# Two sums of a branch layer on VectorE, sigmoids ahead of a weight split, and biased attention with bias and row extreme in one operation

## The reference

```python
# na: 16 heads of 64, 256 queries by 256 keys
s = einsum(q, k) * 64 ** -0.5
s = where(col_mask, s + bias, NEG_INF)          # a bias per head
o = softmax(s) @ v
# branches: four branches of the same normed input, summed under sigmoid gates
s_swa = where(window, q @ k * 64 ** -0.5 + rel_bias, NEG_INF)   # 4 heads, softmax with a sink
s_fox = where(causal, q @ k * 64 ** -0.5 + cum_q - cum_k, NEG_INF)   # 4 heads
g = sigmoid(z_gate)                                             # 4 gates of width 1024
merged = g[0] * p_conf + g[1] * p_sc + g[2] * p_swa + g[3] * p_fox
x = x + merged @ w_out
```

## Time and profile before

| | |
|---|---|
| median of 3 runs | 3464.23 us |
| the profiled execution, its time | 3465.64 us |
| its span, first to last instruction | 3463.8 us |
| granted TensorE clock, mean | 0.983 of full |
| PE (TensorE) busy | 3390.5 us, 98% |
| DVE (VectorE) busy | 2606.3 us, 75% |
| ACT (ScalarE) busy | 1653.2 us, 48% |
| POOL (GpSimd) busy | 203.2 us, 6% |

### The profile page before, as it was taken

One profiled execution on the slowest core, in us unless ns is written; L12 is line 12 of the kernel. 1 busy time (PEld: TensorE's weight loads), 2 busy tenths in 40 slices (PEclk: granted clock), 3 DMA queues, 4 the chain that ended last, 5 costly groups with the idle time before them and its releaser, 6 DMA issues. The chain is left out here.

```text
span 3463.8 us, 59540 instructions
## 1 busy us (share of the span) xinstructions
PE 3390.5 (98%) x23844; PEld 3130.5 (90%) x23844; DVE 2606.3 (75%) x2909; ACT 1653.2 (48%) x1753; POOL 203.2 (6%) x156
## 2 busy tenths in 40 slices
PE   8999999999899999999999999999999999999999
PEld 7999998998699998699999989999999999999998
DVE  7778778775677777577877887777778777777876
ACT  4464444443545444444546444544445444444544
POOL 0000012000000000000000000000341000025100
PEclk9999999999899999899999999999999999999999
DMA  6543385554254554155554335455434545553454
GB/s 247 192 182 122 123 230 179 196 183 146 74 199 178 195 188 153 49 192 186 193 192 173 122 124 202 174 193 193 168 137 165 190 184 197 188 183 129 164 196 168
DMA packets 98937, 592.88 MB, mean 171 GB/s; under 512 B 25684, under 2 KB 26836, under 8 KB 27736
## 3 DMA queue, kind: packets, MB, share of 16 engines
q1 hardware_dynamic: 97280, 586.34, 47.5%
q10 hardware_dynamic: 1496, 4.20, 0.4%
HBM read 588.40 MB, written 2.11 MB: 170 GB/s over the span
## 5 line engine op out<-in xcount | busy, mean ns | idle before, releaser
L1654 DVE TENSOR_TENSOR low<-raw,high 128x2048 fp32r<-128x2048 f32 x531 | 1236.8, 2332 | 229.2 <-ACT high L1180 226.7
L1180 ACT ACTIVATE high<-raw 128x2048 fp32r<-128x2048 f32 x550 | 1049.1, 1910 | 654.5 <-PE acc L445 359.1
L574 PE MATMUL wide<-xs,high 128*128 128x512 f32 x3840 | 1339.3, 391 | 5.9 <-DVE low L1654 5.9
L575 PE MATMUL wide<-xs,low 128*128 128x256 f32 x3840 | 1083.4, 282 | 0.0
L574 PEld LDWEIGHTS wide<-xs,high 128*128 128x128 f32 x3840 | 721.4, 188 | 154.6 <-issue 4.0
L575 PEld LDWEIGHTS wide<-xs,low 128*128 128x128 f32 x3840 | 726.5, 189 | 0.0
L443 PE MATMUL acc<-ends,high 128*128 128x256 f32 x2112 | 588.9, 279 | 0.0
L444 PE MATMUL acc<-ends,high 128*128 128x256 f32 x2112 | 588.8, 279 | 0.0
L445 PE MATMUL acc<-ends,low 128*128 128x256 f32 x2112 | 588.8, 279 | 0.0
L443 PE MATMUL wide<-xs,high 128*128 128x256 f32 x1912 | 550.3, 288 | 13.9 <-DVE low L1669 11.4
L444 PE MATMUL wide<-xs,high 128*128 128x256 f32 x1912 | 540.7, 283 | 0.0
(11 more groups left out here) (229 smaller groups left out, 3596.8 us busy)
## 6 DMA issues: line engine op xcount, KB each, us to landing
raw<-stream SPq DMA_DIRECT2D x550, 1024.0 KB, 4.8
work<-rpb SPq DMA_DIRECT2D x16, 256.0 KB, 7.3
work<-bias_shifted ACTq DMA_DIRECT2D x2, 1024.0 KB, 4.8
cst<-consts SPq DMA_DIRECT2D x1, 1050.0 KB, 11.4
x<-x_in SPq DMA_DIRECT2D x1, 1024.0 KB, 4.9
raw<-stream SPq DMA_DIRECT2D x2, 512.0 KB, 7.2
work<-bias_by_distance ACTq DMA_DIRECT2D x2, 512.0 KB, 4.9
bias_shifted<-work ACTq DMA_DIRECT2D x1, 1024.0 KB, 3.9
```

Of the source, the lines that this page charges most:

```text
L574: nc.tensor.matmul(out[:, n, :, :], wh, xs[:, :, k, :], start=(k == 0), stop=False, skip_group_check=True)
L575: last = nc.tensor.matmul(out[:, n, 0, :], wl, xh[:, k, :], start=False, stop=(k == KC - 1), skip_group_check=True)
L1180: nc.scalar.activation(high[:, s % HIGH, :], raw[:, s % RAW, :], ACT.Copy).then_inc(high_ready, 1)
L1654: v.tensor_tensor(low[:, s % LOW, :], raw[:, s % RAW, :], high[:, s % HIGH, :].bitcast(F32), ALU.subtract).then_inc(low_ready, 1)
```

## The change

Four things, in the `na` layer and in both branch layers:

- **Biased attention.** The scale by 1/8 goes into the query gain: `par("na_q")`, `swq` and `fxq` are multiplied once, by five operations of one column at the program's start, and the cumulated sums of `fox` lose their factor 8. Bias and row extreme are then one operation per 256 columns, `tensor_tensor_reduce`: it writes (scores + bias) times a factor, and accumulates the minimum (or maximum) of what it writes. In `na` and `fox` the factor is -1 and the extreme a minimum, so that the accumulator is the negated maximum, and ScalarE's exponent gets `scale=-1`. The four `swa` heads keep the positive sign and the maximum, since a sink has to be compared with it.
- **Two sums.** `br_m += act3(5)` and `br_m += act3(6)` go from GpSimd to VectorE, the first between `lows(s + 27)` and the variance, the second between `lows(s + 29)` and the gate of slab 30. The semaphore `added` and the waits for it go.
- **Sigmoids ahead of a high half.** On ScalarE, `ahead(s + 15)`, the high half of slab 18, goes behind `gate(2)` and `gate(3)`.
- Everything else stays as it was, the slabs and their order too.

```diff
@@ scalar, attention: exponents @@
-                                last = nc.scalar.activation(probs[h % 4][:, tt, :], acc[h % 4][:, tt, :], ACT.Exp, bias=st[:, tt:tt + 1],
+                                last = nc.scalar.activation(probs[h % 4][:, tt, :], acc[h % 4][:, tt, :], ACT.Exp, bias=st[:, tt:tt + 1], scale=sign,
@@ scalar, branches @@
                 exponents(3)
-                ahead(s + 15)
                 gate(2)
                 gate(3)
+                ahead(s + 15)
@@ vector, attention (na): largest @@
-                    if bias is not None:
-                        added = bias(h)
-                        k = added.shape[-1]
-                        rows = b.rearrange("p a (r k) -> p (a r) k", k=k)
-                        link(v.scalar_tensor_tensor(rows, rows, scale, added, ALU.mult, ALU.add))
-                    v.tensor_reduce(st[:, 0:2], b, AX_X, ALU.max, negate=True).then_inc(logits_ready, 1)
+                    if bias is None:
+                        v.tensor_reduce(st[:, 0:2], b, AX_X, ALU.max, negate=True).then_inc(logits_ready, 1)
+                        return
+                    for tt in range(TT):
+                        added = bias(h, tt)
+                        rows = b[:, tt, :].rearrange("p (r k) -> p r k", k=added.shape[-1])
+                        last = v.tensor_tensor_reduce(rows, rows, added, -1.0, -NEG, ALU.add, ALU.min, st[:, tt:tt + 1])
+                    last.then_inc(logits_ready, 1)
@@ vector, branches: largest @@
-                        added = backwards(toe[:, :, h, :]) if h < SWA_HEADS else con("fxmask").rearrange("p (a t) -> p a t", a=TT)
                         dve.wait_ge(s_done, c.up(s_done))
-                        link(v.scalar_tensor_tensor(b, b, 64 ** -0.5, added, ALU.mult, ALU.add))
+                        for tt in range(TT):
+                            if h < SWA_HEADS:
+                                last = v.tensor_tensor_reduce(b[:, tt, :], b[:, tt, :], backwards(toe[:, tt, h, :]), 1.0, NEG, ALU.add, ALU.max, mx[:, tt:tt + 1])
+                            else:
+                                last = v.tensor_tensor_reduce(b[:, tt, :], b[:, tt, :], con("fxmask", tt * T, T), -1.0, -NEG, ALU.add, ALU.min, st[:, tt:tt + 1])
                         if h < SWA_HEADS:
-                            link(v.tensor_reduce(mx, b, AX_X, ALU.max))
+                            link(last)
                             v.tensor_scalar(st[:, 0:2], mx, par(f"sink{l}", h), -1.0, ALU.max, ALU.mult).then_inc(logits_ready, 1)
                         else:
-                            v.tensor_reduce(st[:, 0:2], b, AX_X, ALU.max, negate=True).then_inc(logits_ready, 1)
+                            last.then_inc(logits_ready, 1)
@@ vector, branches @@
                         if last:
-                            dve.wait_ge(added, 2 * l + 2)
@@
                 lows(s + 27)
+                link(v.tensor_tensor(br_m, br_m, act3(5), ALU.add))
                 q = variance(T, 2 * P)
@@
                 lows(s + 29)
+                link(v.tensor_tensor(br_m, br_m, act3(6), ALU.add))
                 gate(s + 30, 15)
@@ vector, the program's start @@
             dve.wait_ge(params_loaded, 16)
+            for name in ["na_q"] + [f"{n}{l}" for n in ("swq", "fxq") for l in range(LAYERS_2)]:
+                link(v.tensor_scalar(par(name), par(name), 64 ** -0.5, None, ALU.mult))
@@ gpsimd @@
-                for br in (1, 2):
-                    pool.wait_ge(low_ready, s + 24 + br + LOW + 1)
-                    if br == 2:
-                        pool.wait_ge(added, 2 * l + 1)
-                    nc.gpsimd.tensor_tensor(br_m, br_m, act3(4 + br), ALU.add).then_inc(added, 1)
```

More of the change, by code:

```diff
@@ L252, in build @@
         merged = sem("merged")
-        added = sem("added")
         pool_step = sem("pool_step")
@@ L1253, in ffn, with attention @@
                 ahead(s0 + FFN_SLABS - 1)
-            def attention(heads, kind):
+            def attention(heads, kind, sign=1.0):
                 probs, probsT = buffers[kind]
@@ L1407, in na @@
                 ahead(s + 9, 2)
-                step = attention(NA_HEADS, "na")
+                step = attention(NA_HEADS, "na", -1.0)
                 step(0)
@@ L1511, in exponents @@
                             last = nc.scalar.activation(probs[h % 4][:, tt, :], acc[2 * (i % 2) + h % 2][:, tt, :], ACT.Exp, bias=st[:, tt:tt + 1],
+                                                            scale=1.0 if h < SWA_HEADS else -1.0,
                                                         accum_out=st[:, 2 + tt:3 + tt])
@@ L1847, in ffn, with attention @@
                     low_part(KC - 1, gain)
-            def attention(heads, kind, scale=None, bias=None):
+            def attention(heads, kind, bias=None):
                 probs, _ = buffers[kind]
@@ L2113, in na @@
                 dve.wait_ge(bias_masked, NA_HEADS)
-                step = attention(NA_HEADS, "na", NA_DIM ** -0.5, lambda h: backwards(na_b[:, h].rearrange("p a r k -> p (a r) k")))
+                step = attention(NA_HEADS, "na", lambda h, tt: backwards(na_b[:, h, tt]))
                 step(0)
@@ L2277, in branches @@
                 link(v.tensor_tensor_scan(br_l, con("ones", 0, 1, FOX_HEADS).to_broadcast([FOX_HEADS, T]), br_x, 0.0, ALU.mult, ALU.add))
-                v.tensor_scalar(br_cum, br_l, 8.0, None, ALU.mult).then_inc(vec_step, 1)
+                v.tensor_scalar(br_cum, br_l, 1.0, None, ALU.mult).then_inc(vec_step, 1)
                 c.up(vec_step)
-                own(v.tensor_scalar(br_ncum, br_l, -8.0, None, ALU.mult), norm_ready)
+                own(v.tensor_scalar(br_ncum, br_l, -1.0, None, ALU.mult), norm_ready)
                 probs, _ = buffers["branches"]
```

## The result

The changed kernel took 3439.57 us (median of 6 runs, 3433.16 to 3444.14) against 3464.05 for the kernel before (6 runs): a ratio of 0.9931, interval 0.9917 to 0.9946. It is faster by 24.5 us. I had forecast 3451, so a gain of 13; the range ended at 3441. The direction was right and the size was not.

What follows compares the result with a forecast made beforehand. TensorE, in flight 98% of the span, was taken as the bound, so savings count only where it waits. Terms 4.9 + 2.1 + 1.4 + 5.0 = 13.4 us from the median 3464.2 gave 3451 us, range 3441 to 3462.

Steps and rivals of the forecast that it cites:

- Sigmoids first: Slab 16 of both branch layers: `branch` starts 2.9 us earlier and TensorE's whole wait goes, 2 x 2.43 = 4.9 us.
- The term for the clock behind it: Behind slab 16's removed wait: ten matmuls regained at full clock, 1.1 us per layer, 2.1 in all, bounds 0 and 2.1.
- the clock does not come back: Rival: the half-clock stretches behind slab 16's wait have another cause; gain 11.3 us, so 3454; chance 0.18.
- With no wait I take it that the clock stays: Slab 16, both branch layers: without TensorE's wait, the half-clock stretch behind it goes, worth 2.1 us.
- The fused operation: `na` attention: bias and maximum cost 0.90 us per head in place of 1.34, lower bound 0.84, upper 1.36.
- full fixed cost: Rival: every VectorE instruction pays it, so `na` bias and maximum cost 1.16 us per head; sum 10.3, 3455; chance 0.20.
- at half rate: Rival: accumulation runs like the scan, 1.36 us per head; `na` term -0.3, sum 8.1, 3457.5; chance 0.12.
- at a quarter rate: Rival "slower": the fused operation is a slow program, 2.66 us per head in `na`; 3473; chance 0.04.
- The term of `na`: `na` attention: twelve heads where VectorE sets the pace gain 5.3 us, four bring 0.2, less 0.5: 5.0, between -0.3 and 6.0.
- The two sums: Ends of both branch layers: POOL's 3.9 us blocking of VectorE goes, TensorE's wait shrinks by 0.7: 2 x 0.7 = 1.4 us.
- TensorE waits about 1.7 us once per layer: Sign for the sums: one TensorE wait of that length remains ahead of the last branch's second bank.
- Nothing from the branch layers' scores, and nothing from the scalings: VectorE waits 14.4 us for those scores itself; the five start scalings fall into its 2.54 us wait for `x`.

Runs made afterwards that it cites:

- sum2_late: The changed kernel with the second sum behind the gate of slab 30 in place of ahead of it: 3439.4 us, ratio 0.994 to the kernel before.
- sig_layer1: The kernel before with the two sigmoids moved first in the first branch layer only: 3454.46 us, ratio 0.9975.
- na_pad1: The changed kernel with one more one-column VectorE operation per head of `na` attention: 3438.39 us, ratio 0.9936 to the kernel before.
- na_pad3: The changed kernel with three more one-column VectorE operations per head of `na` attention: 3443.57 us, ratio 0.995 to the kernel before.

## Why the prediction was wrong in size

By traces, the change is worth the following. The number of traces stands in brackets, and each length is a mean.

| stretch | without the edit | with it | gain | forecast |
|---|---|---|---|---|
| `na` attention and 60 matmuls behind | 59.9 (10) | 51.2 (6) | 8.7 | 5.0 |
| slab 16, first layer | 20.9 (7) | 16.6 (13) | 4.3 | 3.5 |
| slab 16, second layer | 16.1 (7) | 11.8 (13) | 4.3 | 3.5 |
| second layer, scores to slab 15, by the first layer's edit | 115.2 (7) | 110.7 (13) | 4.5 | 0 |
| ends of both layers, as in `sum2_late` (two sums) | 67.7 (10) | 67.0 (9) | 0.7 | 1.4 |

The sum is 22.5 us, against 24.5 measured; the rest is within the scatter. `mla`, with the same range in both kernels, is left out.

- **Sigmoids first.** The mechanism and the 2 x 2.43 = 4.9 us came as told: the wait is gone in both layers, and `branch` starts right after its gate. The term for the clock behind it was 2 x 1.1. It measured 1.9 us per layer (4.3 less 2.4). I had counted the missing matmuls of one 3 us window (by 18 and 28, of which some only reach into the window). The stretch behind the wait is 3.4 us long in all fourteen cases, and at half of the clock that costs 1.7. The rival "the clock does not come back" is refuted: behind the 26 slabs 16 without the wait no such stretch follows.
- **The step that failed most** is "With no wait I take it that the clock stays: 2 x 1.1 = 2.1 us", as the whole account of the clock. It was right where it stood, but I priced the half clock only directly behind a removed wait. `sig_layer1` shows it in another place, 500 to 600 us later: 4.5 us on the mean of all traces, in code that wasn't touched. My sum had no term for that. The traces point to where the scores start on the grid of the clock, which the edit shifts; that was not tested, so the cause is argued and not shown.
- **The fused operation.** 0.72 us per head, below my lower bound of 0.84. The bound added 0.09 for the accumulator's read, as on ScalarE; on VectorE the read starts together with the next operation, which follows at 0.34 and 0.38 us. By `na_pad1` that was worth 1.1 us. The rivals with a full fixed cost, at half rate and at a quarter rate are all refuted by the timeline. The formula of the Trainium skill (VectorE: DVE Perf Modes, § The TRN2 errata) gave an estimate of 0.85 for two such operations, or 1.16 with reads. The trace has less from start to start: an operation lasts 0.42 to 0.46 us, but the next starts 0.34 or 0.38 behind it. The halved rate of the Trainium skill (Vector Engine (DVE) Microarchitecture Reference, § 7) is stated for two SBUF sources. With the scores in PSUM it doesn't appear: 447 ns for 256 columns, against 678 for the scan.
- **The term of `na`.** With my price, 5.2 us measured against 5.0 forecast for the attention itself. What I missed is the stretch of 13.7 us at half clock that begins in its last 3 us and lies over the 60 matmuls behind it (902.7 to 916.3 before). It cost 4.1 us in this pair and 2.6 on the mean of the traces. I hadn't looked behind the stage. With the fused operation it was absent in every trace, with the old ones present in seven of ten, once in part. Its cause stays open. `na_pad3`, with the fused operation at nearly the old pace, didn't bring it back in three traces, but none of them had the stage at the position where the old operations show the full stretch. And no kernel had the pace of now with the old operations.
- **The two sums.** "TensorE waits about 1.7 us once per layer" was close, at 2.0, and POOL's blocking of VectorE is gone as told. In nine traces with the sums so placed there are eighteen such ends. In three of them no half clock follows, and each is 0.65 to 0.7 us shorter than the mean without the edit: my 0.7. In the other fifteen a stretch of 3.4 us at half clock follows the wait of 2.0 us, and the gain is 0.6 us for both layers together in place of 1.4. The two waits of 1.1 and 1.3 us were followed by none in all twenty ends of the ten traces without the edit. What is late next was here not another engine, but the clock.
- **Nothing from the branch layers' scores, and nothing from the scalings**: right. The five scalings took 0.91 us (3.29 to 4.20) within the wait for `x`. VectorE still waits 15.6 us for those scores.
- **The sums as written.** The bounds of my four terms give at most 4.9 + 2.1 + 1.4 + 6.0 = 14.4 and at least 4.9 + 0 + 1.4 - 0.3 = 6.0, so 3450 to 3458 from the median of before. The 3446 to 3456 of the prediction don't come out of them. The rivals' times start from the profiled execution (3465.6) and the forecast from the median (3464.2), so the rivals stand 1.4 us too high beside it. Neither matters for the outcome: no value within these bounds reaches 24.5.

By the table, the forecast of 13.4 becomes 22.5 by these steps: 4.5 in the second layer's scores, 2.6 in the tail of `na`, 1.6 more of clock behind the two removed waits (on the mean of the traces), 1.1 by the price of the operation, and 0.7 less at the ends. So of the 9.1 us by which my terms were short, 8.0 are clock (the loss at the ends taken off) and 1.1 are the price of the operation.

The runs as a whole also show more clock, but can't be split by cause in this way. The mean time times the mean granted clock is 3406.8 us for the kernel before (76 runs, 3462.5 at 0.9839) and 3397.3 for the changed one (12 runs, 3439.4 at 0.9878), so this product accounts for about 10 of the 23 us between the means. But in `na` it hardly falls, from 61.60 x 0.83 = 51.1 to 51.30 x 0.99 = 50.8, though the padded kernels show that VectorE's pace is what shortened the attention there: where another engine sets the pace, time at half clock isn't time lost.

## What to carry to other kernels

Read the granted clock along with the waits, over the stage that you change and over the one behind it. In a kernel whose TensorE is in flight 98% of the time, a wait of 2.4 us cost 4.3, and about half of a gain was clock that came back, part of it 500 us behind the edit. Then lay two traces of the same kernel over each other before you explain a stage: here `mla` differed by 5 us between executions of one kernel. A stage whose half-clock stretches depend on where it starts can gain or lose by any edit ahead of it, so such a gain belongs to this program and not to the edit. And one wait of 2.0 us was followed by half clock in 15 of 18 cases, a pair of 1.1 and 1.3 us in none of 20.

## What the runs showed of the hardware

- A VectorE operation with an accumulator lets its successor start together with the read of the accumulator (0.34 us after its own start, for 256 columns). The read of 0.14 us added nothing to VectorE's path, neither between two such operations nor ahead of the reciprocal: two operations with their reads took 0.72 us.
- One stretch of 3.4 us at half clock went with TensorE's wait of 2.4 us in all fourteen cases and with that of 2.0 us in 15 of 18. It began between 0.3 us ahead of the wait's end and 1.6 us behind it. With the pair of 1.1 and 1.3 us there was none in 20.
- In every trace the changes of the granted clock lie on one even grid, which lies differently in each execution. The same 790 matmuls took 108.9 to 116.7 us, and their length went with the point in a step of the grid at which they started.
- A VectorE subtraction of 128x2048 that began 0.56 us after GpSimd's addition of the same size ended 2.15 us after it, in all eight cases of two traces of the kernel before. It lasted 6.19 us in place of 2.29, as if it had stood until GpSimd was done.
- How much of a stage with narrow products runs at half clock differs between executions of one kernel (`mla` 17.1 and 27.3 us in both kernels). In the 76 runs of the kernel before, time and mean clock go together with a correlation of -0.96, so the clock is the main part of the scatter.
